# Query projection: the low half of the weight splits goes from VectorE to GpSimd, and the second choice of experts begins inside the projection

## What is computed

```python
def block(hb):                                  # 128 tokens
    q = (hb @ w_query).reshape(PEER_BLOCK, PEER_HEADS, 2, D_KEY // 2)
    s = jnp.einsum('thpc,hpnc->thpn', q, sub_keys)
    top_s, top_i = lax.top_k(s, PEER_TOPK)      # 16 of 128, twice
    ...
    g = jax.nn.softmax(best_s, axis=-1)
    u_sel = jnp.take(u, idx, axis=0)
    a = jax.nn.gelu(jnp.einsum('thkd,td->thk', u_sel, hb), approximate=False)
    v_sel = jnp.take(v, idx, axis=0)
    return jnp.einsum('thk,thkd->td', (g * a), v_sel)
```

## Time and profile before

| | us |
|---|---|
| median of 3 runs (lowest, highest) | 3219.47 (3218.58, 3221.12) |
| the profiled execution, its own time | 3221.12 |
| its span | 3219.3 |
| PE busy | 2159.3 (67%) |
| DVE busy | 1710.9 (53%) |
| ACT busy | 869.3 (27%) |
| GpSimd busy | 792.8 (25%) |
| DMA queue 0 (gathers and GpSimd's other transfers) | 612.85 MB, 47.4% of 16 engines' span |

### The profile page before, as it was taken

How to read it: one execution, slowest core, us unless ns; L and a number is a source line. 1 busy time by engine, 2 the same in 40 slices (tenths; PEclk the granted TensorE clock), 3 DMA queues, 4 the chain that set the end, 5 groups by cost and what they waited for, 6 DMA issues and landing times.

```text
span 3219.3 us, 30897 instructions
## 1 busy us (share of the span) xinstructions
PE 2159.3 (67%) x12338; PEld 1479.6 (46%) x12338; DVE 1710.9 (53%) x2746; ACT 869.3 (27%) x1327; POOL 792.8 (25%) x680
## 2 busy tenths in 40 slices
PE   4799998989998999899989982222223232232235
PEld 1566676878787777667658871000000000000001
DVE  2336546664655654343345679556555655565430
ACT  1333444444444444554545421000000000000000
POOL 1011100000000000000000025555555555555552
PEclk8999999999999999999989996566666666666667
DMA  8898964557764554342324687999999999999998
GB/s 306 300 309 264 302 211 137 183 167 253 221 184 138 157 161 148 114 130 93 123 88 154 211 296 305 417 421 422 421 422 422 422 421 422 422 421 421 422 422 340
DMA packets 243594, 901.01 MB, mean 280 GB/s; under 512 B 20374, under 2 KB 45228, under 8 KB 177004
## 3 DMA queue, kind: packets, MB, share of 16 engines
q0 software_dynamic: 94208, 612.85, 47.4%
q1 hardware_dynamic: 148768, 285.58, 27.7%
q10 hardware_dynamic: 476, 0.62, 0.1%
HBM read 894.78 MB, written 2.10 MB: 279 GB/s over the span
## 4 chain that ended last, share of the span: by engine, by line
PE 53%; DMA 31%; DVE 9%; ACT 3%; issue 2%; POOL 1%; DVEq 0%; ACTq 0%; POOLq 0%
PE pp L1718 46%; DMA late<-in_peer_v,MI 10%; PE tp L1718 5%; DMA P<-in_peer_v,MI 5%; DMA ring<-in_peer_v,MI 5%; DMA x<-in_peer_v,MI 4%; DVE wL L1067 2%; DMA SY<-in_peer_v,MI 2%; PE tp L1721 2%; DMA late<-in_w_mod 1%; DMA ring<-in_peer_w_query 1%; ACT wH L583 1%; DMA ring<-in_w_in 1%; DMA P<-in_w_mod 0%; DMA x<-in_x 0%
## 5 line engine op out<-in xcount | busy, mean ns | idle before, releaser
L1067 DVE TENSOR_TENSOR wL<-ring,wH 128x1024 fp32r<-128x1024 f32 (+3 forms) x504 | 582.1, 1161 | 600.7 <-ACT wH L583 597.0
L1718 PE MATMUL pp<-wH,hH 128*128 128x512 f32 (+3 forms) x1888 | 749.8, 397 | 39.4 <-DVE wL L1067 28.6
L1718 PE MATMUL pp<-wH,hL 128*128 128x512 f32 (+3 forms) x1888 | 718.2, 380 | 0.0
L1718 PE MATMUL pp<-wL,hH 128*128 128x512 f32 (+3 forms) x1888 | 717.9, 380 | 0.0
L583 ACT ACTIVATE wH<-ring 128x1024 fp32r<-128x1024 f32 (+3 forms) x504 | 505.5, 1009 | 475.1 <-PE pp L1718 313.7
L1718 PEld LDWEIGHTS pp<-wH,hH 128*128 128x128 f32 x1888 | 360.0, 191 | 183.7 <-issue 71.8
L1718 PE MATMUL pp<-late,S 128*32 128x512 f32 x736 | 230.5, 897 | 295.8 <-DMA P<-in_peer_v,MI 76.0
L1718 PEld LDWEIGHTS pp<-wH,hL 128*128 128x128 f32 x1888 | 359.1, 190 | 64.0
L1718 PEld LDWEIGHTS pp<-wL,hH 128*128 128x128 f32 x1888 | 360.5, 191 | 55.7 <-issue 1.2
L1718 PE MATMUL pp<-P,S 128*32 128x512 f32 x376 | 267.4, 878 | 149.1 <-DMA x<-in_peer_v,MI 76.2
L1718 PE MATMUL pp<-x,S 128*32 128x512 f32 x376 | 166.8, 888 | 219.9 <-DMA ring<-in_peer_v,MI 219.9
(11 more groups left out here) (302 smaller groups left out, 2996.8 us busy)
## 6 DMA issues: line engine op xcount, KB each, us to landing
ring<-in_w_in SPq DMA_DIRECT2D x288, 512.0 KB, 4.5
ring<-in_w_out SPq DMA_DIRECT2D x96, 512.0 KB, 4.7
P<-in_w_mod POOLq DMA_DIRECT2D x85, 512.0 KB, 5.1
late<-in_w_mod SPq DMA_DIRECT2D x64, 512.0 KB, 9.4
SY<-in_w_mod POOLq DMA_DIRECT2D x43, 512.0 KB, 5.4
ring<-in_w_in SPq DMA_DIRECT2D x48, 368.0 KB, 4.6
ring<-in_peer_w_query SPq DMA_DIRECT2D x32, 512.0 KB, 4.9
ring<-in_w_in SPq DMA_DIRECT2D x24, 344.0 KB, 3.2
```

What stands on the lines that cost most here:

```text
L1067: tt(lo, raw, hi.bitcast(F32), ALU.subtract).then_inc(*tick("dve_lo", *names))
L1718: return e.matmul(o, l, r, start=start, stop=stop, skip_group_check=skip)
```

## The change

Three edits. Splits of projection 6 are done by GpSimd: DVE's `split` returns after counting, and GpSimd gets one of its own, with the same operation and the same wait for ACT, under a new semaphore `pool_lo`; it walks the same entries, so its splits stand in its queue among its loads and gathers. The scores and the choice of i = 1 are opened after piece 17 (two pieces into the third query group) instead of ahead of dot 16. And each piece of groups 2 and 3 pumps lane X by 0.42, so that this choice moves on beside dots 0 to 15.

```diff
--- before.py
+++ after.py
@@ -330,10 +330,15 @@
             yield from pump(1.25, 0, 0)
         if g == 1 and pc == 7:
             yield "drain", "X"
+        if q == 17:
+            yield "scores", 1
+            yield "skip_pair",
+            yield "open", "X", "choose", 1
         if g >= 2:
             yield "dot", 0, 8 * g - 16 + pc
+            yield from pump(0.42, 0, 0)
     for i in range(8):
-        if i < 7:
+        if 0 < i < 7:
             yield "scores", i + 1
             yield "open", "X", "choose", i + 1
         for j in range(0 if i else 16, 32):
@@ -401,7 +406,7 @@
         handles = {}
         for name in ("pe_piece", "pe_turned", "pe_bias", "pe_side",
                      "act_hi", "act_stored", "act_x", "act_y", "act_h", "act_side",
-                     "dve_lo", "dve_stored", "dve_x", "dve_y", "dve_h", "dve_side",
+                     "dve_lo", "pool_lo", "dve_stored", "dve_x", "dve_y", "dve_h", "dve_side",
                      *[f"mod_in{i}" for i in range(11)], "const_in", "pos_in", "x_in", "meta_in", "forget_in", "ffn_in", "decay_in", "turned_in", "out_done",
                      *[f"ring_in{i}" for i in range(NS)], *[f"expert_in{i}" for i in range(NG)]):
             handles[name] = sem(name)
@@ -1058,6 +1063,8 @@
             def split(p, q):
                 n, c0, wd, pc = PIECES[p][q]
                 r, k = next(loads), next(cut)
+                if p == 6:
+                    return
                 raw = heads(ring[:, r % NS, 0:2 * wd], 2)
                 hi, lo = (heads(b[k % NB][:, 0:2 * wd], 2) for b in (wH, wL))
                 w.wait_ge(*at("hi", k))
@@ -2228,6 +2235,18 @@
         def gpsimd(e, w):
             gathers = itertools.count()
 
+            loads, cut = itertools.count(), itertools.count()
+
+            def split(p, q):
+                n, c0, wd, pc = PIECES[p][q]
+                r, k = next(loads), next(cut)
+                if p == 6:
+                    raw = heads(ring[:, r % NS, 0:2 * wd], 2)
+                    hi, lo = (heads(b[k % NB][:, 0:2 * wd], 2) for b in (wH, wL))
+                    w.wait_ge(*at("hi", k))
+                    e.tensor_tensor(lo, raw, hi.bitcast(F32), ALU.subtract).then_inc(
+                        *tick("pool_lo", ("lo", k), ("ring used", r)))
+
             def load(sem, to, src, *names):
                 e.dma_start(to, src).then_inc(*landed(sem, *names))
 
@@ -2291,6 +2310,10 @@
                         load("pos_in", rb0[32 * q + 1:32 * q + 32, 8 * q:8 * q + 8], I["rel_bias"][0:31, :],
                              *([("positions",)] if q == 3 else []))
                     load("x_in", x[:, :, :], x_d, ("x",))
+                elif what == "split":
+                    split(*a)
+                elif what == "sub_keys":
+                    next(loads), next(loads)
                 elif what == "open":
                     lanes.open(*a)
                 elif what == "step":
```

## The result

| | before | after |
|---|---|---|
| median of 20 runs each (lowest, highest), us | 3221.47 (3217.53, 3225.72) | 3226.73 (3222.34, 3230.38) |
| the profiled execution, its own time | 3221.12 | 3224.06 |
| its span | 3219.3 | 3222.2 |
| DVE busy | 1710.9 | 1702.8 |
| GpSimd busy | 792.8 | 888.2 |

The ratio is 1.0015, interval [1.0008, 1.0021]: the changed kernel is slower by about 4.8 us (2.6 to 6.8). The forecast was 3226.5 us.

The account below looks back on a forecast made before the run. The DMA gather stream bounds the kernel, so its unbroken start sets the end. The 13 us hole goes, but sixteen gathers take 20 us more: +7.0 us, median 3226.5 us; own range 3218 to 3236, with rivals 3206 to 3238.

Parts of the forecast that it names:

- The hole, 13 us: DMA stop near 1989.2 to 2002.2 us, gather 32 awaiting choice 1; moving the choice ahead removes it, worth 13 us.
- The split on GpSimd, 2.3 us: Cost of one low-half split moved to GpSimd: 2.3 us taken, bounded by 1.22 and 4.1.
- The rival with 3.0 us and loaded code: GpSimd slower yet: splits of 3.0 us, a few us of code loading at the start; 3241 us, chance 0.10.
- The block in both directions: GpSimd splits or gathers and DVE instructions with two SBUF inputs stop each other; chance 0.55.
- side by side: Rival: splits and dots don't block each other, only gathers wait; cycle 4.2 us, 3206.5 us, chance 0.22.
- only GpSimd waits: Rival: dots start freely and splits wait for them; cycle 4.7 us, 3214 us, chance 0.13.
- The cycle, 5.6 us: Each split-and-gather pair beside the projection: split 2.3, dot 2.28, gather 0.9, gap 0.1; twelve such cycles.
- The start, 4 us: Group 0's pieces and choice 0's begin come 4 us later, norm loads standing behind splits 0 and 1; bounds 3 to 6.
- Choice 0 beside the splits: Eight groups of two-input operations, 0.7 us each, quarrel with splits and push split 18 from 1883.6 to 1886.8.
- The end, +7.0 us: Gathers 32 on follow from 2009.2 instead of 2002.2: hole gone, but the sixteen gathers beside the projection take 20 us more.
- the three cases: Chances against a 0.2% (6.4 us) bound: faster 0.24, same 0.34, slower 0.42.
- a piece at half speed, 5.8 us: PE piece beside the first gathers, if the granted clock falls: 5.8 us, which the 5.6 us cycle would just bear.

Follow-up runs that it names:

- e2: Changed kernel with all splits back on DVE, only scores and choice 1 moved; 3206.39 us against 3221.34 for the kernel before, ratio 0.9953.
- The kernel with 18: e2 with gathers 16 and 17 kept to the first five buffers, ring buffers coming in at 18; 3203.86 us against 3221.27 before, ratio 0.9945.
- e3: Changed kernel with dots 0 to 15 replaced by a plain one-input sum of the gathered rows; 3211.99 us against 3221.34 before, ratio 0.9966.
- e7: Changed kernel with splits 0 to 17 on GpSimd and 18 to 31 on DVE; 3211.30 us against 3221.27 before, ratio 0.9970.

## Why the prediction was right

**The hole, 13 us.** Right. It is 13.4 behind the first gather (before less e2), and gather 32 no longer waits. The step held for the reason given: the numbers are ready in time. The margin was nothing, though. The step that makes the last numbers of choice 1 ends at 1994.71, and GpSimd is done with gather 31 at 1994.70:

```profile
1994.45 0.26 DVE L1607 CAST MI<-MI 128x32 uint32<-128x32 f32 x1
```

The kernel with 18, which has no split on GpSimd, shows the same 0.31 us of idle time ahead of its gather 32, so the small margin does not come from the block. The DMA had gathers in hand and stayed at 1.02.

**The split on GpSimd, 2.3 us.** Measured 2.35 to 2.41 alone, 2 to 5% above the 2.3 that was taken. The page GPSIMD Engine Reference of the Trainium skill (section 3.1) had led to an estimate of 2.25; the trace lies 4 to 7% above it. The rival with 3.0 us and loaded code falls: the first two splits together took 4.77 us, no more than any other two.

**The block in both directions.** Right, and the step on which everything hung. The prediction had gathers for one direction only the earlier trace rows; the dots of 2.94 and 4.52 us, the split of 3.80 and the untouched sums of e3 show the other. By the Trainium skill, SBUF — State Buffer, section "Who interferes with whom", the shared port pair is "an exclusive lock"; the trace agrees, 5.36 us for three works that take 2.36, 2.2 and 0.8 us one after the other. The conversion of 1.30 us is a case beyond the two-input rule as the prediction cites it. A distance of 5.36 fits neither the rival "side by side" (4.2) nor "only GpSimd waits" (4.7).

**The cycle, 5.6 us.** Too long by 0.24. The sum counted a gather's whole 0.9 us and a gap of 0.1 behind a dot's whole 2.28. In the trace the gather ends 0.81 to 0.82 us after the dot, and the split starts 0.02 after the gather. Over twelve cycles this is 2.9 us: gather 14 went at 1958.32, where the prediction said 1961.2. Gather 15 went 71.5 us behind the first, against 51.8 before, the 20 us that were said.

**The start, 4 us.** Measured 4.8 for the begin of choice 0, counted from piece 0, inside the bounds of 3 to 6. Its steps held one by one. Piece 2 came 9.66 us after piece 0 instead of 6.55, 3.1 late where 3 was said, after 2.87 us of waiting for GpSimd's split; and the next row of ACT, which answers to the 1844.20 of the earlier trace rows, stands 19.58 us after piece 0 instead of 15.49, 4.1 late:

```profile
1836.60 0.39 PE L1725 MATMUL tp<-hH,wH 128*128 128x256 f32 x1 [2.87 <-POOL wL L2247]
```

```profile
1846.52 1.07 ACT L588 ACTIVATE wH<-ring 128x1024 fp32r<-128x1024 f32 x1 [4.13 <-DMA ring<-in_peer_w_query]
```

That split 18 stood at 1886.68 (1886.8 said) and the first gather at 1889.20 (1889 said) is in part luck: this execution reached piece 0 at 1826.94, 1.8 us ahead of the one on which the sum was made. Counted from piece 0 the first gather is 6.4 us late, where the prediction had 4.5.

**Choice 0 beside the splits.** Eight groups at 0.7 us, 5.6 in all, were expected on 18.3; it took 24.7 us from 1860.66 to 1885.4, so 6.4. The sum was near and its shape was not: one group of three operations holds 4.4 of it, and the conversion of 1.30 us, which has one input and was not counted, another 1.1. The first two rows below stand beside the splits of 1875.53 and 1878.41 and take 5.9 us; the last two, with GpSimd idle, are the same work in 1.45:

```profile
1875.44 2.97 DVE L1592 TENSOR_TENSOR U<-MI,CW 128x256 f32<-128x256 f32 x2
1878.44 2.92 DVE L1595 TENSOR_TENSOR U<-U,MI 128x512 f32<-128x512 f32 x1
...
1882.55 0.76 DVE L1592 TENSOR_TENSOR U<-MI,CW 128x256 f32<-128x256 f32 x2
1883.34 0.69 DVE L1595 TENSOR_TENSOR U<-U,MI 128x512 f32<-128x512 f32 x1
```

**The end, +7.0 us.** Measured 4.8 by the ratio (2.6 to 6.8), 4.7 from piece 0 to the span's end, and 6.6 from piece 0 to the last gather (1369.81 less 1363.24). The sum stands just above the interval. Two of its terms were mis-sized and partly cancel: the way to the first gather was 2.0 us longer than said, the cycles 2.9 shorter. What is left between them and the 4.8, some 1.3 us, is less than the spread of single executions. That the median came out within 0.3 us of the forecast is luck: the change was 2 us smaller than said, and the kernel before ran at 3221.47 in the larger set of runs, 2 us above the three that were shown. Of the three cases, slower by over 0.2% had the highest chance, and there the result doesn't fall: 4.8 us is 1.6 inside the bound of 6.4.

**Two slips in the working.** The range counts the start as 1 us less or 2 more (3 and 6 us about 4), although its sentence says 3 either way; with 3 it would begin at 3216.5. And a piece at half speed, 5.8 us, would not fit a cycle of 5.6. The clock did not fall that far, so nothing came of it.

**What stays open.** Behind the first gather e7 needs 3.2 us more than the choice alone, though none of GpSimd's splits stands there; no run separates this from the spread between executions. And the 2.7 us of the start that splits 2 and on cost were not divided further.

## What to carry to other kernels

Before work is moved from VectorE to GpSimd, look at what VectorE does in that stretch. Beside instructions that read two tensors from SBUF, GpSimd's time is added to theirs (5.36 us a cycle here). Beside the plain sum and the selection of the top 16, which read one, it was free; beside a short conversion, which also reads one, it was not. So look at the records of the instructions at hand. Where GpSimd also issues the gathers that feed those instructions, the three line up into a cycle that sustains itself, and reordering the queue didn't break it here. And a change of two parts should be costed and tried as two: here one was worth 15 us and the other took 20, and the engine that seemed too full for the first had waits that the steps fitted into.

## What the runs showed of the hardware

- This waiting is not idle time in the profile. It is inside the record: a dot of 2.28 us shows up to 5.04, a conversion of 128 x 64 numbers, 0.19 alone, up to 2.32. The sign is a mean that rises; the first twelve dots, beside GpSimd's splits, average 3.4 us.
- A gather's issue is stopped by an instruction of VectorE with two inputs in SBUF as a split is, and ends 0.80 to 0.82 us after it. The steps of the top-16 selection over 128 scores, which read one tensor of scores, keep their 0.28 to 0.30 us beside a split, and the split its 2.37 (1909.87 of the changed kernel's timeline).
- The DMA's busy share and its rate parted: from 1900 to 1940 the engines show 0.87, though 290 to 300 GB/s are 0.70 of the 422 of the stream. One gather and one piece of weights in 5.36 us are 1.573 MB, 293 GB/s, so the bytes are those expected, and the share counts time in which the transfers ran below the stream's rate. The prediction's 0.7 was right for the rate and wrong for the share.
- TensorE waited 0.7 to 2.2 us for a split ahead of the pieces from 1900 on. The granted clock of the three windows from 1900 to 1960 was 0.83, 0.90 and 0.76, means between its levels of 1.2 and 2.4 GHz; from 1884 to 1944 it was 0.89, against 0.91 before. The pieces still fit into 5.36 us.
